# Latent pages of a paged attention turned by VectorE after an on-chip transfer, instead of by TensorE

## What is computed

```
def step(carry, phys):
    c_blk = cache_ckv[layer, phys]
    kp_blk = cache_kpe[layer, phys]
    kn_blk, v_blk = _decompress(c_blk, w_ukv, g_kn)
    return _merge(carry, _attn_partial(qn, qp, kn_blk, kp_blk, v_blk, None)), None
def _decompress(c_kv, w_ukv, g_kn):
    kv = einsum('btc,chd->bthd', c_kv, w_ukv)
    return _rmsnorm(kv[..., :NOPE], g_kn), kv[..., NOPE:]
```

## Time and profile before

| | |
|---|---|
| runs | 1332.09, 1332.03, 1331.44 us; median 1332.03 |
| profiled execution | 1327.66 us |
| its span in the profile | 1325.6 us, mean granted TensorE clock 0.981 |
| busy | PE 1271.7, DVE 716.2, ACT 455.3, POOL 152.7 us |
| DMA | 81.48 MB in 82995 packets, mean 61 GB/s |

### The profile page before, as it was taken

One profiled execution on the slowest core, in us unless ns is written; L12 is line 12 of the kernel. 1 busy time (PEld: TensorE's weight loads), 2 busy tenths in 40 slices (PEclk: granted clock), 3 DMA queues, 4 the chain that ended last, 5 costly groups with the idle time before them and its releaser, 6 DMA issues. The chain is left out here.

```text
span 1325.6 us, 25998 instructions
## 1 busy us (share of the span) xinstructions
PE 1271.7 (96%) x9479; PEld 740.7 (56%) x9479; DVE 716.2 (54%) x1781; ACT 455.3 (34%) x1108; POOL 152.7 (12%) x182
## 2 busy tenths in 40 slices
PE   6999999889999999999999989999999999989898
PEld 4545677656666666655545545665545455454343
DVE  4001448654566656565767776777666666530331
ACT  3001354233343434342445433343444444310320
POOL 0000326400010202024302320000000000000000
PEclk9999999899999999998999998999999999999899
DMA  6422121111111111310331114311333212001000
GB/s 213 161 79 54 34 64 33 52 38 33 30 36 44 39 32 39 74 50 20 93 101 46 41 37 133 131 38 37 103 119 111 79 55 71 34 0 36 16 16 36
DMA packets 82995, 81.48 MB, mean 61 GB/s; under 512 B 18947, under 2 KB 76612, under 8 KB 82869
## 3 DMA queue, kind: packets, MB, share of 16 engines
q1 hardware_dynamic: 80452, 73.87, 18.5%
q10 hardware_dynamic: 2416, 5.96, 1.3%
HBM read 75.72 MB, written 4.07 MB: 60 GB/s over the span
## 5 line engine op out<-in xcount | busy, mean ns | idle before, releaser
L499 PE MATMUL PS<-wk,c_T 128*128 128x512 f32 x1024 | 494.5, 606 | 0.0
L624 DVE TENSOR_REDUCE ssq<-sq__69 128x8 f32<-128x512 f32 x256 | 175.2, 684 | 183.1 <-ACT sq__69 L553 181.9
L499 PEld LDWEIGHTS PS<-wk,c_T 128*128 128x128 f32 x1024 | 176.6, 192 | 152.0 <-issue 139.6
L553 ACT ACTIVATE sq__69<-PS 128x512 f32<-128x512 f32 x256 | 152.6, 596 | 315.8 <-PE PS L499 315.3
L1482 PE MATMUL PS<-xnT,w_ring 128*128 128x276 f32 x416 | 102.6, 404 | 0.0
L1320 PE MATMUL PS<-w_ring,xnT 128*128 128x424 f32 x256 | 95.7, 531 | 0.9 <-DVE xnT L976 0.9
L1482 PEld LDWEIGHTS PS<-xnT,w_ring 128*128 128x128 f32 x416 | 78.9, 193 | 21.2 <-issue 4.1
L455 PE MATMUL PS<-cst,c_ring 128*128 128x128 f32 x512 | 79.6, 278 | 6.1 <-DVE dots_s L619 4.7
L455 PEld LDWEIGHTS PS<-cst,c_ring 128*128 128x128 f32 x512 | 60.3, 143 | 44.7 <-issue 40.2
L1320 PEld LDWEIGHTS PS<-w_ring,xnT 128*128 128x128 f32 x256 | 48.7, 194 | 45.3 <-issue 45.2
L2690 PE MATMUL PS<-w_g,nT 128*128 128x512 f32 x128 | 56.0, 594 | 0.0
(11 more groups left out here) (533 smaller groups left out, 1872.1 us busy)
## 6 DMA issues: line engine op xcount, KB each, us to landing
c_ring<-in_cache_ckv SPq DMA_DIRECT2D x256, 128.0 KB, 2.8
w_ring<-in_w_in SPq DMA_DIRECT2D x4, 1696.0 KB, 12.5
w_ring<-in_w_in SPq DMA_DIRECT2D x9, 512.0 KB, 5.1
r_ring<-in_cache_kpe SPq DMA_DIRECT2D x256, 16.0 KB, 1.8
w_o<-in_w_out SPq DMA_DIRECT2D x8, 512.0 KB, 4.2
w_g<-in_w_ple_gate SPq DMA_DIRECT2D x8, 512.0 KB, 3.6
xn<-in_x_prompt SPq DMA_DIRECT2D x4, 512.0 KB, 11.0
w_ring<-in_w_in SPq DMA_DIRECT2D x2, 1024.0 KB, 6.0
```

Source lines behind the costliest of these rows:

```text
L499: mm = pe.matmul(PS[:, NORM[v % 2], :], c_T[:, u % 2, k, t * P:(t + 1) * P], wk[:, k], start=(k == 0), stop=(k == 1))
L553: nc.scalar.activation(sq_[:, v % 2, :], PS[:, NORM[v % 2], :], ACT.Square).then_inc(no_sb, 1)
L624: dve.tensor_reduce(ssq[:, u % 2, t * H:(t + 1) * H], sq_[:, v % 2, :].rearrange("p (h c) -> p h c", h=H), AX.X, ALU.add).then_inc(red_sb, 1)
```

## The change

- **Turning.** The eight identity matmuls of a step and their two copies out of PSUM are gone. Instead ScalarE issues four on-chip transfers a step (`latent_blocks`), each from all 128 partitions of a ring slot, 64 of the 256 columns, to 32 partitions of a block tile `c_blocks`; position 4p+x comes to partition p. VectorE then turns 32x32 blocks with two `transpose` instructions into `c_T` (now two tiles, `c_T0` and `c_T1`, by the parity of the step). The latent columns lie on the partitions in another order, and `wk` is loaded in that order by eight transfers on SP in place of ScalarE's cut, so `qp` follows it.
- **When.** The transfers of step u+2 stand in slot 2 of step u on ScalarE, ahead of the square, and wait for the landed pages and for the transposes of step u+1 (`ct_sb`), since there is one block tile. The transposes of u+1 stand in slot 1 of step u on VectorE, ahead of merge and reduction.
- **Squares stay in PSUM.** ScalarE squares the NORM bank in place, VectorE reduces from PSUM, and norms wait for the reduction two groups back (`red_sb`) instead of the square.
- **Dots copy.** It moves from VectorE (slot 1) to ScalarE (slot 3, behind the exponentials of u-1), with one buffer instead of two. The turn of the rotary keys waits for it (`rp_sb`).
- **Sizes.** The page ring has five slots instead of four, two pages' steps are loaded ahead in the input stage instead of three, PREP_SLOTS is 2 instead of 5 (TAIL_SLOTS three more).
- **Output stage.** The turn of the sample rows and its two copies move ahead of the first gate product; `mixed(3)` ahead of `normed(1)`; tiles lie at other places in SBUF.

```
-RING = 4
+RING = 5
-PREP_SLOTS = 5
+PREP_SLOTS = 2
-        ahead_pages = 3
+        ahead_pages = 2
+        def latent_blocks(eng, u, groups_c):
+            eng.wait_ge(c_in[u % RING], 16 * GT * (u // RING + 1))
+            if u >= 1:
+                eng.wait_ge(ct_sb, u)
+            for g in groups_c:
+                eng.dma_start(c_blocks[32 * g:32 * g + 32].rearrange("p x t c -> p (x t c)"),
+                              c_ring[:, slot_of[u], :, g * (KVL // 4):(g + 1) * (KVL // 4)]).then_inc(b_in, 16)
...
         def pages_pe():
-                for t in range(GT):
-                    mm = pe.transpose(PS[:, TURN, t * P:(t + 1) * P], c_ring[:, u % RING, t, k * P:(k + 1) * P], ident)
-                mm.then_inc((k0_ps, k1_ps)[k], 1)
...
             def turn_r(u):
                 pe.wait_ge(r_in[u % R_RING], 16 * GT * (u // R_RING + 1))
-                pe.wait_ge(k1_sb, u + 1)
+                if u >= 1:
+                    pe.wait_ge(rp_sb, u)
...
                 if v >= 2:
-                    pe.wait_ge(no_sb, v - 1)
+                    pe.wait_ge(red_sb, v - 1)
...
         def pages_act():
+            def dotted(u):
+                if u >= 1:
+                    act.wait_ge(eq_sb, u)
+                act.wait_ge(rp_ps, u + 1)
+                nc.scalar.copy(dots_s[:].rearrange("p x c -> p (x c)"), PS[:, TURN, P:3 * P]).then_inc(rp_sb, 1)
...
-                nc.scalar.activation(sq_[:, v % 2, :], PS[:, NORM[v % 2], :], ACT.Square).then_inc(no_sb, 1)
+                nc.scalar.activation(PS[:, NORM[v % 2], :], PS[:, NORM[v % 2], :], ACT.Square).then_inc(no_sb, 1)
...
-                if t == 2 and ahead:
-                    turned_c(u + 1)
-                if t == 3 and u >= 1:
-                    weights(u - 1)
+                if t == 3:
+                    if u >= 1:
+                        weights(u - 1)
+                    dotted(u)
+                if t == 2 and u + 2 < NSTEP:
+                    latent_blocks(act, u + 2, range(4))
                 square(u, t)
...
         def pages_dve():
             def turned_c(u):
-                dve.wait_ge(k1_ps, u + 1)
-                dve.tensor_copy(c_T[:, u % 2, 1, :], PS[:, TURN, :]).then_inc(k1_sb, 1)
+                dve.wait_ge(b_in, 16 * 4 * (u + 1))
+                if u >= 2:
+                    dve.wait_ge(rp_ps, u - 1)
+                    dve.wait_ge(no_ps, (u - 1) * GT)
+                for k in range(2):
+                    ins = dve.transpose(c_T[u % 2][:, k].rearrange("p (t a x) -> p t x a", t=GT, x=GT),
+                                        c_blocks[:].rearrange("p x t (k c) -> p k t x c", k=2)[:, k])
+                ins.then_inc(ct_sb, 1)
...
                 if t == 1:
-                    dotted(u)
+                    if ahead:
+                        turned_c(u + 1)
                     if u >= 2:
                         merge(u - 2)
...
-                if t == 3 and ahead:
-                    turned_c(u + 1)
...
         def _(pe):
                 projected(2, 1)
+                pe.wait_ge(mt_act, 3)
+                pe.wait_ge(mt_dve, 3)
+                pe.wait_ge(own_sb, 1)
+                s_turn(s_rows[:, C_GA:NAT], OUT_M, ms_ps)
                 gated(0, 0)
                 gated(0, 1)
-                pe.wait_ge(mt_act, 3)
-                pe.wait_ge(mt_dve, 3)
-                s_turn(s_rows[:, C_GA:NAT], OUT_M, ms_ps)
+                mixed(3)
                 normed(1)
-                mixed(3)
```

More of the change, by code:

```diff
@@ L251, in build @@
         ms = place("ms", [P, 4])
+        turned_at = place.at
+        c_T0 = place("c_T0", [P, 2, GT * P])
         ring_at = place.at
-        c_T = place("c_T", [P, 2, 2, GT * P])
+        c_ring = place("c_ring", [P, RING, GT, KVL + 1])
+        blocks_at = place.at
+        c_blocks = place("c_blocks", [P, GT, GT, KVL // 4])
+        c_T = c_T0, place("c_T1", [P, 2, GT * P])
+        rope_at = place.at
         r_T = place("r_T", [P, P])
@@ L256, in build @@
         w_ring_at = t1_at + 4 * (NT * D + KD * TEXT)
-        assert place.at <= w_ring_at
-        pages_at = place.at = w_ring_at
-        c_ring = place("c_ring", [P, RING, GT, KVL + 1])
+        slot_bytes = 4 * GT * (KVL + 1)
+        assert ring_at + 3 * slot_bytes >= w_ring_at and rope_at - 4 * 2 * GT * P <= w_ring_at + 4 * KD * (NAT // 4)
         tmp_at = place.at
@@ L485, in values @@
                     pe.wait_ge(ring_ready, 1)
+                pe.wait_ge(c_in[u % RING], 16 * GT * (u // RING + 1))
                 pe.wait_ge(ew_sb, u + 1)
@@ L494, in norms @@
                 if t == 0:
-                    pe.wait_ge(k1_sb, u + 1)
+                    pe.wait_ge(ct_sb, u + 1)
                 if v >= 2:
-                    pe.wait_ge(no_sb, v - 1)
+                    pe.wait_ge(red_sb, v - 1)
                 for k in range(2):
-                    mm = pe.matmul(PS[:, NORM[v % 2], :], c_T[:, u % 2, k, t * P:(t + 1) * P], wk[:, k], start=(k == 0),
+                    mm = pe.matmul(PS[:, NORM[v % 2], :], c_T[u % 2][:, k, t * P:(t + 1) * P], wk[:, k], start=(k == 0),
                                    stop=(k == 1))
                 mm.then_inc(no_ps, 1)
-            turn_c(0, 0)
             yield
-            turn_c(0, 1)
             yield
             for u, t in slots:
-                ahead = u + 1 < NSTEP
                 if t == 0:
@@ L516, in pages_pe @@
                         values(u - 2)
-                if t == 2:
-                    if ahead:
-                        turn_c(u + 1, 0)
-                    if u >= 1:
-                        turn_scale(u - 1)
-                if t == 3 and ahead:
-                    turn_c(u + 1, 1)
+                if t == 2 and u >= 1:
+                    turn_scale(u - 1)
                 norms(u, t)
@@ L574, in turned_weights @@
                 nc.scalar.copy(ew[:], PS[:, MISC, at_t]).then_inc(ew_sb, 1)
-            turned_c(0)
+            latent_blocks(act, 0, range(4))
             yield
+            latent_blocks(act, 1, range(4))
             yield
             for u, t in slots:
-                ahead = u + 1 < NSTEP
                 if t == 0:
@@ L743, in _ @@
                     weights(n)
+                    if n == 2:
+                        sp.wait_ge(xT_ps, NT + 1)
+                        for g in range(4):
+                            for k in range(2):
+                                c0 = g * (KVL // 4) + 32 * k
+                                nope = io["w_ukv"][c0:c0 + 32, :].rearrange("i (h c) -> i h c", h=H)[:, :, 0:NOPE]
+                                sp.dma_start(wk[32 * g:32 * g + 32, k].rearrange("p (h c) -> p h c", h=H), nope
+                                             ).then_inc(wk_in, 16)
                     if n == 5:
@@ L2480, in build @@
         sums = place("sums", [P, BS])
-        pT = place("pT", [P, 2, TALL])
+        pT = nat[:, 0:2, 0:TALL]
         mT_a = place("mT_a", [P, KD, P])
@@ L3018, in _ @@
                 ins.then_inc(at_sb, 1)
+                act.wait_ge(ms_ps, 1)
+                nc.scalar.copy(msT[:, 0:4, :], turned_of(OUT_M, NS)).then_inc(ms_act, 1)
                 gated(0)
+                mixed(3)
                 act.preload_act_table_set(LN_EXP)
                 added(2)
-                act.wait_ge(ms_ps, 1)
-                nc.scalar.copy(msT[:, 0:4, :], turned_of(OUT_M, NS)).then_inc(ms_act, 1)
                 turned_n(1)
-                mixed(3)
                 act.wait_ge(os_ps, 1)
```

84 lines of the change are left out of this document (32 added, 52 removed).

## The result

| | before | after |
|---|---|---|
| median of the runs | 1332.06 us (1331.44 to 1332.83, 4 runs) | 1370.67 us (1363.71 to 1373.81, 4 runs) |
| profiled execution, its span | 1327.66, 1325.6 us | 1370.99, 1369.2 us |
| granted TensorE clock, mean | 0.981 | 0.963 |

The change makes the kernel slower: ratio 1.029, 95% interval 1.026 to 1.032. The forecast was 1289 us with a range of 1264 to 1316, and gave slower a chance of 0.06. It has the wrong sign and misses by 82 us.

A forecast was written before the change was run, and what follows sets the result against it. TensorE, busy 1271.7 of 1325.6 us, was taken as the bound. -55.7 - 3 + 7 + 4 + 2 + 3 = -42.7 from 1327.66 gave 1285, plus 4.4 to the median: 1289 us, range 1264 to 1316.

The forecast's parts named there:

- The work removed: Whole page stream: taking the page turns off TensorE saves 64 steps x 0.87 us, -55.7 us.
- The path: Page-only stage: ScalarE's issues, square, exponentials and dots copy delay the rope turn 0.3 us a step, +7 us.
- I take 0.69, because every operation on 512 elements in the trace has it: VectorE: each of two 128x512 block transposes a step takes 0.69 us, at the upper end 1.23.
- I take 0.55 with the gap: ScalarE's sequencer: four transfer issues a step at 0.55 us each hold it 2.2 us a step.
- In the mixed stages two slots last 7.8 us and hold it.: Mixed stages before the page-only stage: two slots are long enough to hide the delay from ScalarE's issues, no cost.
- up to 0.9 us late once a step: 8 steps: Attention stage: VectorE's transposes and merging delay the next unit's maximum, +4 us; the latent stage before it, +2 us.
- The lower clock: Between 275 and 1146 us: a granted clock below 0.98 was named as a sign of a wrong forecast, without a cost.
- The transfers: Block transfers, 512 KB a step: the last of four lands in 3 us, bounds 2.8 and 7.8; wanted 6.6 us after issue.
- rival 3: Blocks come late: the one block buffer's loop of 3.95 us plus landing lengthens steps, +21 us, 1353 us; chance 0.06.
- Norms waiting for the reduction: NORM banks free only after VectorE's reduction: wait hidden by the other bank's matmuls, no cost; uncovered, about 1.5 us a slot.
- Start of the stream: First blocks 1.3 us later, second blocks hold the last prepared slot some 1.7 us: +3 us.
- Output stage: Sample rows' turn ahead of the first gate product fills a TensorE wait, and L2717 waits for the third sum alone: -3 us.

## Why the prediction was wrong, point by point

**The work removed** was counted right: 512 turns left TensorE. In the kernel with neither transfers nor the merge behind the transposes the page stream alone runs at 8.87 us a step (201.7 us for 91 slots), where the forecast had 8.89 for a step without turns.

**The path** in the page-only stage was followed right: transposes, issues, square, exponentials, dots' copy, rope turn. Its durations were too short. "I take 0.69, because every operation on 512 elements in the trace has it" for a transpose: it takes 1.09 us, in the upper half of the bounds. The reason was false too: in the kernel before, products of two 128x512 operands take 0.82 to 1.01 us in the mean (L2354, L2355, L2170). The 1.24 us, an estimate from the Trainium skill ("VectorE: DVE Perf Modes", the three transpose paths: four times its 311 ns, which are for bfloat16), was nearer than the row that I trusted, as the trace of the changed kernel shows. "I take 0.55 with the gap" for an issue: the fours shown above took 2.92 and 3.3 us, 0.73 to 0.82 each; the median of all 256 is 0.67 and single ones reach 2.0. The rows it rests on the earlier trace rows are of transfers of another shape. It is not the traffic that makes the median: the eight block issues of the kernel without transfers, issued by 264 us, have the same 0.67.

**The step that failed** is this one: "In the mixed stages two slots last 7.8 us and hold it." I divided a long step by its slots and took the quotient as slack. In these stages ScalarE and VectorE serve a second chain with its own dates. In the attention stage it is maximum, exponentials, turn; it was priced at "up to 0.9 us late once a step: 8 steps", +4 us, of VectorE's load alone. Single waits were up to 3.4 us, 23.6 in all, and the clock behind them fell to 0.90. The stage by the same 34 slots (from the start of its first slot's norms to that of the next stage's), in the kernel before, the changed one, and the one with neither transfers nor the merge behind the transposes (length of the stretch, then busy time of each engine as in the earlier trace rows, TensorE first; the granted clock is the third number from the end):

```profile
806.50:932.70 126.20, 123.07 (x733) 76.98 (x732) 99.15 (x299) 50.15 (x153) 0.00 (x0) 1.00 0.26 83
...
808.40:966.60 158.20, 132.19 (x692) 78.41 (x690) 105.98 (x300) 51.55 (x158) 0.00 (x0) 0.91 0.46 90
...
783.40:921.20 137.80, 121.58 (x692) 70.32 (x690) 105.77 (x301) 50.37 (x157) 0.00 (x0) 1.00 0.22 69
```

With 8.5 steps of turns gone (7.4 us), the change cost this stage 39 us where the forecast had 4, and 19 of them are there without any issue or transfer. All stages, cut at the same slots, as differences to the kernel before in the profiled executions (the forecast's column is its 0.87 us a step plus its terms for the stage):

| stage | forecast | changed kernel | neither transfers nor merge behind |
|---|---|---|---|
| recurrences, 92 slots | -20 | +0.6 | -12.8 |
| prompt's latents, 35 slots | -6 | +2.9 | -5.2 |
| its attention, 34 slots | -3 | +32.0 | +11.6 |
| page stream alone, for 88 slots | -12 | +5.5 | -18.5 |
| start, the three moved slots, output stage | -2 | +2.6 | -1.8 |
| sum | -43 | +43.6 | -26.7 |

Of the 86 us between forecast and changed kernel, some 64 lie in the three mixed stages, which the failed step took as slack, 35 of them in the attention stage (14 us of the 64 may be the merge's waits, see below); 18 lie in the page-only stage, where the merge is the main term that was missing.

The lower clock is a term that the forecast did not have, and mentioned only as what would make it wrong. Between the changed kernel and the one without transfers it is 24 of the 46 us. It follows the long waits: with the issues behind the squares the clock was 0.980 again, and as much time went into idle instead.

**The term that was missing** is the merge (27.3 us of TensorE's waits, 13.3 of them in the page-only stage). I placed transposes and "0.47 of merging" ahead of slot 1's reduction and asked only who waits for the reduction. TensorE's turn of the scales waits for the merge itself (`acc_sb`) one slot later. Moving the merge gave 24 us where no transfer ran, and nothing while the issues still stood behind the transposes.

**The transfers** were sized right (2.8 to 7.8 us bounds; 3.6 to 4.1 us median landing in the five kernels with all transfers for which the trace has it), and rival 3, the only one on the right side, was wrong about this kernel: VectorE waits 6.0 us for blocks. Its loop does exist. It became the limit as soon as the issues were moved: 72.8 us of VectorE's waits by SyncE, 32.2 us behind the squares. "By row and rule alike the sum stays" for the traffic is not borne out as it stands: with three quarters of the packets 17 us went, though how much of that is the shorter time of issuing stays open.

**The small terms** held, one of them in part by luck. Norms waiting for the reduction: no cost in the kernel before. Start of the stream: +3 was forecast as 1.3 for the first norms and 1.7 for late second blocks; the first norms alone came 3.1 us later (261.6 against 258.5). Output stage: from the last norms to the end 176.6 us against 179.8, so -3.2 for -3.

**How the sum comes out**, by medians: 1300 us with neither transfers nor the merge behind the transposes, against 1289 forecast; +24 for the merge: 1324; +29 for issues with a quarter of the traffic: 1353; +17 for the rest of it: 1371. The 11 us left at the bottom are 16 by the profiled executions, and by the table they lie in the attention stage (15 us short of the forecast) and the recurrences (7), while the page-only stage is 6 better than forecast, having no wait for the dots' copy. All of the exponentials' wait of 16.2 us, 3.1 before, is in that attention stage. Whether the transposes on VectorE or the dots' copy on ScalarE lengthen it was not parted.

## What to carry to other kernels

A buffer that one engine frees, a second refills by issuing and the first reads again is a loop through two in-order engines. Wherever its waits stand, whatever stands behind them in either queue waits too; so price a move by both queues at once, and expect single moves to show nothing (0 and +3 us here) where the pair shows 34. Slack is not the length of a stage over its slots: for every instruction behind the added one on its engine, write down who waits for it and from when. And work taken from the engine at the bound is a gain only if no one who releases it becomes later: here 512 instructions left TensorE, and it came out 39 us slower.

## What the hardware showed unexpectedly

VectorE's transpose of 128x512 in float32 takes 1.09 us from and to SBUF, where the reductions and copies of that size take 0.67 to 0.69 as group means.

An issue from ScalarE costs it 0.62 us even for 128 packets and 0.67 for 512 (medians), and up to 2.0 us at times; compute behind it waits.

The queue of the 256-byte packets between parts of SBUF took 32 ns of a DMA engine for each packet (20.1% of 16 engines over 1369.2 us, for 137584 packets, 131072 of them these), and 26 ns where the same transfers were issued two by two behind the squares (16.2% of 1371.6 us). The other queue's packets went from 49 to 56 ns each in their company (18.5% of 1325.6 us for its 80452 packets in the kernel before, 21.3% of 1369.2 us for 82628 now), and back to 49 without the transfers.

A wait of 2.7 us on TensorE can be paid more than once: the granted clock was 1.00 from 860 to 869 us, and 0.83 from 873, where the wait ended, to 883, that is, part of it at the lower level of 1.2 GHz; the norms behind the wait took 2.62 us where those ahead of it took 1.94. Not each wait does it: behind one of 2.4 us that ended at 949 the clock stayed at 1.00.
